# A transformer kernel's odd mixer written out with values projected around its transposes, and its modulation dot products begun in turn 0

## What is computed

```
# modulation: one row of 6*1024 numbers per layer and stream, used in the norms and gates
mod = silu(c) @ ada_w[l] + ada_b[l]
# swiglu of the first block, 2816 hidden columns
(silu(a @ w1) * (a @ w3)) @ w2
# odd mixer: 16 heads of 64, 256 queries over 256 latent keys (with a bias and a neighbourhood mask)
# and 256 context keys
q, k, v = split(h @ w_in, 3);  kc, vc = split(hc @ w_in[:, 1024:], 2)
s = concat([q @ k.T * scale + bias (masked), q @ kc.T * scale])
y = (softmax(s) @ concat([v, vc])) @ w_out
```

## Time and profile before

| | |
|---|---|
| median of 3 runs | 3214.33 us (3209.99 to 3214.36) |
| profiled execution: time, span | 3211.18 us, 3209.4 us |
| PE matmul busy | 2907.0 us, 91% of the span |
| DVE busy | 1186.2 us, 37% |
| ACT busy | 716.4 us, 22% |
| mean granted clock of TensorE | 0.951 |

### The profile page before, as it was taken

One profiled execution on the slowest core, in us unless ns is written; L12 is line 12 of the kernel. 1 busy time (PEld: TensorE's weight loads), 2 busy tenths in 40 slices (PEclk: granted clock), 3 DMA queues, 4 the chain that ended last, 5 costly groups with the idle time before them and its releaser, 6 DMA issues. The chain is left out here.

```text
span 3209.4 us, 35102 instructions
## 1 busy us (share of the span) xinstructions
PE 2907.0 (91%) x12470; PEld 1610.6 (50%) x12470; DVE 1186.2 (37%) x2789; ACT 716.4 (22%) x1392; POOL 20.0 (1%) x26
## 2 busy tenths in 40 slices
PE   6999899999999978997996999999887878999997
PEld 3545344444466767884545333333355554444444
DVE  2421587730356647712313233333332322222222
ACT  2332200000255521002332212122122221212121
POOL 0000000000000000000000000000000000000000
PEclk9989999999999989998897999999999888999999
DMA  6122465532222116742013899999521127999995
GB/s 239 68 105 105 178 237 227 235 131 78 101 77 66 47 65 263 301 170 90 14 40 143 345 398 390 393 398 390 225 67 58 59 79 310 393 400 394 401 395 208
DMA packets 101819, 664.29 MB, mean 207 GB/s; under 512 B 10608, under 2 KB 19056, under 8 KB 25072
## 3 DMA queue, kind: packets, MB, share of 16 engines
q1 hardware_dynamic: 99152, 653.84, 52.1%
q0 software_dynamic: 2592, 9.44, 0.7%
HBM read 660.09 MB, written 3.15 MB: 207 GB/s over the span
## 5 line engine op out<-in xcount | busy, mean ns | idle before, releaser
L581 PE MATMUL PB<-A,RING 128*128 128x512 f32 (+1 forms) x1408 | 462.9, 492 | 29.5 <-DMA RING<-ffn_w 11.8
L581 PEld LDWEIGHTS PB<-A,RING 128*128 128x128 f32 x1408 | 271.4, 193 | 221.1 <-issue 184.0
L2101 PE MATMUL PB<-RING,BIG 128*64 128x512 f32 x1536 | 344.2, 597 | 0.0
L614 DVE SCALAR_TENSOR_TENSOR WORK<-RING,MORE 128x1024 f32<-128x1024 f32 x288 | 335.5, 1221 | 19.3 <-ACT MORE L595 10.8
L422 PE MATMUL PB<-BIG,RING 128*128 (+2 forms) x928 | 310.7, 497 | 5.6 <-PEq L549 3.3
L2298 DVE TENSOR_TENSOR BIG<-BIG,PB 64x512 f32<-64x512 f32 x64 | 44.1, 690 | 691.9 <-ACT BIG L2189 691.9
L2133 PE MATMUL PB<-BIG 128*128 128x512 f32 (+1 forms) x544 | 211.8, 512 | 49.2 <-DVE X L2305 45.4
L422 PEld LDWEIGHTS PB<-BIG,RING 128*128 128x128 f32 x928 | 175.9, 190 | 139.3 <-issue 128.7
L2101 PEld LDWEIGHTS PB<-RING,BIG 128*64 128x64 f32 x1536 | 110.4, 138 | 211.1 <-issue 210.8
L2305 DVE SCALAR_TENSOR_TENSOR X<-PB,MODS,X 128x256 f32<-128x256 f32 x408 | 176.5, 479 | 40.6 <-PE PB L2133 38.5
L2133 PEld LDWEIGHTS PB<-BIG 128*128 128x128 f32 x544 | 90.0, 188 | 184.0 <-DVE X L2305 106.5
(11 more groups left out here) (351 smaller groups left out, 3396.6 us busy)
## 6 DMA issues: line engine op xcount, KB each, us to landing
RING<-moe_w SPq DMA_DIRECT2D x288, 1024.0 KB, 8.4
MORE<-moe_w SPq DMA_DIRECT2D x96, 1024.0 KB, 8.6
RING<-ada_rows SPq DMA_DIRECT2D x72, 1024.0 KB, 6.7
RING<-ffn_w SPq DMA_DIRECT2D x66, 1024.0 KB, 4.8
RING<-ada_w SPq DMA_DIRECT2D x17, 1024.0 KB, 6.4
RING<-hg_w_in SPq DMA_DIRECT2D x16, 1024.0 KB, 4.9
RING<-odd_w_in SPq DMA_DIRECT2D x8, 1024.0 KB, 5.0
BIG<-ada_w SPq DMA_DIRECT2D x5, 1024.0 KB, 12.8
```

The lines of the kernel that those rows point to most:

```text
L581: last = pe_.matmul(PB[:, 2 * s + j, 0:t], tile(s, KD, P, j * KD * P)[:, k, :], A[:, k, 0:t], start=k == 0, stop=k == KD - 1)
L614: last = dve_.scalar_tensor_tensor(out=JUNK[:, n % 4, :], in0=RING[:, s, b * D:(b + 1) * D], scalar=1.0, in1=WIDE[:, side // 2, w, :], op0 ...
L2101: last = pe_.matmul(PB[m * CAP:(m + 1) * CAP, 0, :], XGT[:, b, k, slots_of(e % 2)], spot_tile(s, 4, T)[:, k % 4, :], start=k == 0, stop=k ...
```

## The change

Three things are changed.

1. `feed_forward`: the dot products of chunk i are computed in turn i, chunk 0 included. SP's loop issues `w13` of turn i and then the tiles of chunk i; the last chunk (11) is issued behind the first output weights, and its dot products stand at the start of the DVE part of the next `boundary` (new argument `sides`), with a wait of SP for them ahead of `free`.
2. `even_mixer`: `join.dve` stands ahead of the rotary tables.
3. `odd_mixer`: written out for the eight pairs. The transposes of both heads stand together, half of the next pair's values (16 of 32 matmuls) are projected behind them, then both heads are weighed with their matmuls alternating between the two halves of the output partitions, then comes the other half of the values. Queries and keys are staged apart from the values. Maxima and transposed copies are one instruction per head.

```diff
     def boundary(product, gain, layer, shift, scale, t, free, rest, sides=()):
...
+                for s in range(2, 2 + 2 * len(sides)):
+                    sp.wait_ge(*of(f"used{s}", 1))
                 free(sp)
...
         def dve_part(dve):
+            for share in side_shares(sides):
+                side_dots(dve, of, sides, share, 0, 11)
...
     def feed_forward(join, w13, w2, layer, t, context=False, sides=()):
...
                 join.sp(sp)
-                for share in shares:
-                    side_loads(share, 1)
                 with sp.Fori(1, turns) as i:
                     for s in range(2):
                         sp.wait_ge(used[s].sem, used[s].at(i))
                         sp.dma_start(RING[:, s, :], w13[2 * i + s]).then_inc(loaded[s].sem, 16)
-                        side_loads(shares[s], i + 1)
+                        side_loads(shares[s], i)
                 first_rows(sp, w2, turns)
+                for share in shares:
+                    side_loads(share, turns)
...
                 join.dve(dve)
                 dve.wait_ge(sig("wide_silued").sem, sig("wide_silued").at(len(pairs)))
-                for share in shares:
-                    side_dots(share, 0)
                 with dve.Fori(0, turns) as i:
                     for s in range(2):
-                        side_dots(shares[s], i + 1)
+                        side_dots(dve, of, sides, shares[s], i, i)
...
     def even_mixer(join, layer):
...
             def _(dve):
+                join.dve(dve)
                 chain = Chain(dve, sig("dve_step"))
...
                 chain(last)
-                join.dve(dve)
...
     def odd_mixer(join, layer):
...
+                def scores(m):
                     pe.wait_ge(sig("staged").sem, sig("staged").at(m + 1))
+                    for t in range(2):
+                        for i in range(2):
+                            last = pe_.matmul(PB[:, 2 * i + t, :], QB[rows[i], t * P:(t + 1) * P], KB[rows[i]],
+                                              start=True, stop=True)
...
+                def weigh(m):
+                    pe.wait_ge(sig("value_copied").sem, sig("value_copied").at(m + 1))
+                    pe.wait_ge(sig("carried").sem, sig("carried").at(m))
+                    pe.wait_ge(sig("turned").sem, sig("turned").at(2 * m + 2))
+                    for kt in range(NT):
+                        for i in range(2):
+                            last = pe_.matmul(PB[rows[i], 7, 0:S], VB[:, kt, rows[i]], PTB[i][:, kt, 0:S],
+                                              start=kt == 0, stop=kt == NT - 1)
+                    last.then_inc(sig("weighted").sem, 1)
...
+                for m in range(KD):
+                    more = m + 1 < KD
+                    scores(m)
                     if more:
+                        project_queries_keys(m + 1)
+                    flips(m)
+                    if more:
+                        project_values(m + 1, 0)
+                    weigh(m)
+                    if more:
+                        project_values(m + 1, 1)
...
+                        act_.activation(PTB[i][:, :, 0:S], PB[:, 2 * i:2 * i + 2, :].rearrange("p a (b n) -> p (a b) n", b=2),
+                                        ACT.Copy).then_inc(sig("turned").sem, 1)
+                    if m + 1 < KD:
+                        stage(m + 1)
...
     product = hgrn2(boundary(product, vec("norm1", KD, 2 * KD), 1, 0, 1, T, hgrn2_head(1), hgrn2_head(0),
+                              (1, 2)), 1)
```

More of the change, by code:

```diff
@@ L382, in first_rows, with side_shares, side_dots, boundary @@
         sp.dma_start(RING[:, 0, :], w[0]).then_inc(loaded[0].sem, 16)
-    def boundary(product, gain, layer, shift, scale, t, free, rest):
+    def side_shares(sides):
+        spots = [(j, x) for j in range(len(sides)) for x in range(2)]
+        return spots[:len(sides)], spots[len(sides):]
+    def side_dots(dve, of, sides, share, i, chunk):
+        dots = 8 * len(sides)
+        for j, x in share:
+            s, side = 2 + 2 * j + x, sides[j]
+            dve.wait_ge(*of(f"loaded{s}", 16 * (i + 1)))
+            if x == 0:
+                dve.wait_ge(*of("mod_added", len(sides) * (i - 1) + j + 1))
+            for b in range(2):
+                for w in range(2):
+                    n = 8 * j + 4 * x + 2 * b + w
+                    dve.wait_ge(*of("dotted", dots * i + n - 3))
+                    dve_.scalar_tensor_tensor(
+                        out=JUNK[:, n % 4, :], in0=RING[:, s, b * D:(b + 1) * D], scalar=1.0,
+                        in1=WIDE[:, side // 2, w, :], op0=ALU.mult, op1=ALU.mult,
+                        accum_out=DOTS[:, j, n % 8:n % 8 + 1]).then_inc(sig("dotted").sem, 1)
+            dve.wait_ge(*of("dotted", dots * i + n + 1))
+            dve.sem_inc(used[s].sem, 1)
+            if x == 1:
+                dve_.tensor_tensor(MODS[:, side, bass.ds(4 * chunk, 4), :],
+                                   DOTS[:, j, :].rearrange("p (n w) -> p n w", w=2),
+                                   ada_bias(side, 4 * chunk, 4), ALU.add).then_inc(sig("mod_added").sem, 1)
+    def boundary(product, gain, layer, shift, scale, t, free, rest, sides=()):
         at = {name: signal.base for name, signal in signals.items()}
@@ L505, in multiplied @@
                 eng.wait_ge(*of("product_made", KD))
+        for s in range(2, 2 + 2 * len(sides)):
+            used[s].passed(1)
+            loaded[s].passed(16)
+        passed(mod_added=len(sides), dotted=8 * len(sides))
         for s in range(2 if product else 0):
@@ L658, in first_key @@
         return 0 if t < 2 else S
[L662 to L704, removed]
@@ L1377, in odd_mixer, with turned_place @@
         near = con("near")
-        def biased(t, b):
-            return SC[:, 2 * b + t, :]
-        each = 4
+        rows = [slice(i * HD, (i + 1) * HD) for i in range(2)]
+        def turned_place(i, kt):
+            return PB[:, 2 * i + kt // 2, (kt % 2) * S:(kt % 2 + 1) * S]
         with nc.Block() as block:
@@ L1454, in _ @@
                 join.dve(dve)
-                with dve.Fori(0, KD) as m:
-                    chain = Chain(dve, sig("dve_step"), m, each)
+                chain = Chain(dve, sig("dve_step"))
+                for m in range(KD):
                     dve.wait_ge(sig("bias_in").sem, sig("bias_in").at(16 * (m + 1)))
@@ L1461, in _ @@
                             last = dve_.tensor_tensor(BI[:, 2 * i + t, 0:S], BI[:, 2 * i + t, 0:S], near, ALU.add)
[L1462 to L1463 removed]
+                    chain(last)
+                    for i in range(2):
+                        n = 2 * m + i
                         dve.wait_ge(sig("scored").sem, sig("scored").at(n + 1))
```

145 lines of the change are left out of this document (64 added, 81 removed).

## The result

The changed kernel takes 3097.94 us (median of 4 runs, 3096.82 to 3100.11) against 3212.86 us (4 runs, 3209.99 to 3214.36; the three runs of the table ahead of the prediction and one more). The ratio is 0.9649, with a 95% interval of 0.9638 to 0.9661: faster, by 115 us, against a forecast of 3101.

The account below looks back on a forecast made before the run. PE, busy 91% of the span, bounds the kernel, so other engines' edits count only where PE waits. 13.7 + 10.2 + 12.9 + 73.4 = 110.2 us off 3211.2 gives 3101 us; range 3084 to 3128.

Parts of the forecast that it names:

- Feed-forward 0: PE's 11.57 us stop for DVE's first `h` goes, with 2.1 us of slow clock behind it: 13.7 us.
- Feed-forward 1: PE's 8.21 us stop for a weight tile issued late goes, with 2.0 us of clock: 10.2 us.
- The last chunk: Feed-forward end: later chunk tiles and dot products at the boundary hide under the product; cost 0, uncovered 20 and 10 us.
- Ahead of the even mixer: Boundary before rotary tables: PE's 10.10 us stop for ACT goes, with 2.8 us of clock; 12.9 us.
- Period of the odd mixer: Waits hidden, full clock, weighing paired: 23.5 us a pair; seven periods take 164.5 us against 232.08, 67.6 less.
- Weighing: Odd mixer: alternating halves run in pairs at 256 columns, halving 3.88 us for both heads, a gain of 1.94.
- Ends: Odd mixer: first scores skip the values' copy, 0.8 us; last pair takes 18 us, not 24.06, less 1 for clock: 5.
- halves that fail to pair: Rival, odd mixer weighing: no pairing at 256 columns; 13.6 us in periods and 2 in last pair return, 3117; chance 0.12.
- new wait inside the periods: Rival, odd mixer: DVE and ACT chain stays on the path, 20 to 34 us lost, 3121 to 3135; chance 0.12.
- given back in the feed-forwards: Rival, feed-forwards: chunk tiles or output weights come late, 10 to 20 us lost, 3111 to 3121; chance 0.08.
- late instructions: Rival, odd mixer: PE's written-out list is fetched as it runs, PE stands at seams; slower, 3229 at 16 us a pair; chance 0.02.
- Each stop only moves: Rival, whole change: each stop only moves to the next engine, 3205 to 3217 us; chance 0.01.

Follow-up runs that it names:

- the load-order experiment: Kernel before, SP alone changed in both feed-forwards: `w13` of turn 1 issued ahead of loads waiting for DVE, dot products unmoved; 3208.59 us, ratio 0.9993.
- the opposite experiment: Changed kernel with its early dot products, but SP issues the tiles of chunk 1 ahead of `w13` of turn 1; 3120.63 us, ratio 0.9723.
- The experiment head by head: Changed kernel with the eight weighing matmuls of a pair taken one head after the other, not alternating; 3104.33 us, ratio 0.9669.
- by twos: Changed kernel, odd mixer: weighing two matmuls of one head, then two of the other; scores head by head; 3097.24 us, one run.
- the written-out kernel: Kernel before with the odd mixer's loops of PE, ACT and DVE unrolled, order of work unchanged; 3189.46 us, ratio 0.9933.

## Why the prediction was right, step by step

- **Feed-forward 0**, 13.7 forecast: 13.8. The stop of 11.57 is gone, and 2.25 us of PE's busy time with it.
- **Feed-forward 1**, 10.2 forecast: 10.5. The size was right, the reading only in part, and that is luck. I put the stop down to the load alone; the load-order experiment shows that DVE was due 1.6 us earlier, and loads first alone gains 0.8 of these 10.5 us. The sum held only because the change moves both; the prediction did not count on that. The claim that SP stood behind DVE holds (the opposite experiment has the stop for the load back), but it was not the only thing that the stop hung on.
- **The last chunk**, 0 forecast: 0. No new wait for `ffn_w` in either product; the product and the HGRN2 mixer between the feed-forwards take 529.99 us against 529.93.
- **Ahead of the even mixer**, 12.9 forecast: 13.5. The stop of 10.1 is gone, PE's busy time fell by 3.0 where I took 2.8 for the clock, and the last wait for `A` is 0.4 shorter (6.19 and not 6.56).
- **Period of the odd mixer**, 23.5 forecast: 23.40. Clock 1.00, PE busy without a gap, as the signs of being right had it. The chain of DVE was put at 10 to 11.3 us behind the scores and took 10.0 (2347.02 - 2337.02).
- **Weighing**, 1.94 forecast, from rows of the experts with twice the columns: 1.87. That a length of 512 could stand for 256 held. The experiment head by head shows where the gain comes from. The page "TensorEngine Tiling (Array Packing)" of the Trainium skill, section Key Properties, lets different tiles work in parallel; the trace agrees, and shows that how much runs in parallel hangs on the order in the list (1.87, 1.93 and 2.79 us).
- **Ends**, 0.8 and 5 forecast: 0.8 and 6.4. The last pair took 17.67 us, as in the forecast (18); the 1 us that I added for a product at low clock did not come: its 96 records take 20.96 us both before and after. Of the 6.4 us, 1.8 come from scores that now run at full clock (3.79 us before, 1.99 after). What the slow clock still costs lies in the transposes and the weighing, 3.68 us each for what takes 1.91 and 1.95 in a period.
- **The rivals**: no halves that fail to pair, no new wait inside the periods, nothing given back in the feed-forwards, no late instructions. "Each stop only moves" is false for the change as a whole; for either half of the edit in the feed-forward it is true, the stop stays or changes its releaser.

How the 68.3 us of the seven periods divide: 10.2 for the shorter wait ahead of the scores (mostly the table load), 9.4 for the clock when written out only, and the rest, 48.8, for order and pairing. Of these the weighing has 7 x (3.88 - 1.87) = 14.1, of which 7 x (2.79 - 1.87) = 6.4 are the alternation's and the rest comes with both heads standing together; the waits of 1.30 twice and 1.85 once make 7 x 4.45 = 31.2; that leaves 3.5 for the clock from 0.98 to 1.00. No run takes back by itself the separate staging of queries and keys, or the single maximum and copy of a head, so their parts in this aren't known.

## What to carry to other kernels

A stop has every cause that would end within a few microseconds of it: ask of each wait what is due next. In the feed-forward the loads alone and the dot products alone were each worth about 1 us and together 24. Give every wait for another engine independent matmuls to lie under, split in pieces as long as the other engine's work (16 matmuls of 3.7 us over copies of 1.9 us); with the stops gone the granted clock came back as well, here from 0.93 to 1.00. And where work is taken into a wait, look at the granted clock behind it too: in the last pair the slow stretch only came later, over the product. Interleave matmuls that write different halves of the output partitions: here, at 256 columns, by ones or twos they took the time of one half.

## What the runs showed of the hardware that was not expected

- Eight weighing matmuls (16 records) of 256 columns with 64 output columns take 1.87 us alternating, 1.93 by twos, 2.79 with one head right behind the other, 3.88 when a wait and transposes lie between the heads.
- How short stops act on the clock: three a pair (1.30, 1.30, 3.31) gave 0.93 over seven periods, three (1.30, 1.30, 1.85) gave 0.98, one of 1.25 gave 1.00. The clock did not fall in the first two of the seven periods before, nor in the first three of the written-out kernel.
- In the last pair a slow stretch of about 10 us came where the longest stop was 6.39 us, and came too where it was 2.62 us. With the shorter stop it began 4 us later, counted from the scores, and fell over the product (22.74 against 20.96 us for the same 96 records). Why it begins where it does no run shows.
- With the loads of chunk 1 first, a 1 MB weight tile issued behind four chunk tiles of 1 MB held PE until 402.29, 7 us after its issue at 395.29; the median landing of such a tile is 4.8.
